# Streaming encoder step with PEER gathers: h for the dot products moved from PSUM to an SBUF copy, and the row ring from thirteen to twelve

## The reference, cut to what matters

```python
def peer(h, w_q, sub_keys, expert_u, expert_v):
    q = (t @ w_q).reshape(T, 8, 2, 64)
    s = jnp.einsum('thpd,hpnd->thpn', q, sub_keys)
    ts, ti = lax.top_k(s, 16)
    ...
    act = jax.nn.gelu(jnp.einsum('td,thkd->thk', xb, expert_u[idb]), approximate=False)
    return jnp.einsum('thk,thkd->td', gtb * act, expert_v[idb])
```

## Time and profile before

| | |
|---|---|
| runs | 3525.51, 3532.18, 3525.33 us |
| profiled execution, own time | 3508.12 us |
| its span, first to last instruction | 3505.7 us |
| mean granted TensorE clock | 0.825 |
| busy: PE / VectorE / GpSimd / ScalarE | 2387.2 / 2172.2 / 2141.8 / 259.9 us |
| gathers | 2176, 1140.99 MB, 86.0% of 16 DMA engines' span |

### The profile page before, as it was taken

One profiled execution on the slowest core, in us unless ns is written; L12 is line 12 of the kernel. 1 busy time (PEld: TensorE's weight loads), 2 busy tenths in 40 slices (PEclk: granted clock), 3 DMA queues, 4 the chain that ended last, 5 costly groups with the idle time before them and its releaser, 6 DMA issues.

```text
span 3505.7 us, 25147 instructions
## 1 busy us (share of the span) xinstructions
PE 2387.2 (68%) x7990; PEld 890.5 (25%) x7990; DVE 2172.2 (62%) x5644; ACT 259.9 (7%) x506; POOL 2141.8 (61%) x2184
## 2 busy tenths in 40 slices
PE   7123876577875875587978366748798764865498
PEld 6112323121311241123314121412332322111022
DVE  3988278866666775735467777772716787655500
ACT  3000100100000000000100100001010000000000
POOL 0365566656665655666566656565656675666665
PEclk9666898788987967798989688669899886878799
DMA  6587898999899989997897999799789899999998
GB/s 236 222 326 297 297 366 313 366 349 378 320 379 360 350 318 409 410 410 290 309 366 292 372 341 387 291 379 355 288 316 362 339 349 348 369 387 385 370 380 330
DMA packets 331598, 1201.44 MB, mean 343 GB/s; under 512 B 40898, under 2 KB 41290, under 8 KB 329418
## 3 DMA queue, kind: packets, MB, share of 16 engines
q0 software_dynamic: 313344, 1140.99, 86.0%
q1 hardware_dynamic: 17034, 49.94, 3.7%
q10 hardware_dynamic: 1088, 8.91, 0.6%
HBM read 1188.82 MB, written 10.87 MB: 342 GB/s over the span
## 4 chain that ended last, share of the span: by engine, by line
PE 23%; another core or an unknown queue 21%; POOL 18%; DVE 17%; issue 14%; DMA 5%; ACT 2%; ACTq 0%; DVEq 0%; POOLq 0%
POOL rows L590 18%; PE acc L974 11%; DVE rows L1420 8%; PE psA L807 4%; DMA rows<-in_expert_v,idsT 4%; PE psB L917 3%; PE psA L798 2%; DVE work L1149 1%; DMA rows<-in_expert_u,ids 1%; DVE work L1235 1%; DVE work L1228 1%; PE psB L834 1%; DMA w_in_sb<-in_w_in 1%; DVE work L1225 1%
## 5 line engine op out<-in xcount | busy, mean ns | idle before, releaser
L974 PE MATMUL acc<-rows,strip 128*32 128x512 f32 x4352 | 1558.1, 654 | 546.8 <-DMA rows<-in_expert_v,idsT 403.3
L1420 DVE CUSTOM_DVE_ANT_0 rows<-rows,psH 128x1024 f32<-128x1024 f32 x1088 | 1290.9, 1218 | 399.7 <-DMA rows<-in_expert_u,ids 296.3
L590 POOL DMA_INDIRECT rows<-in_expert_v,idsT x1088 | 1100.5, 1011 | 667.3 <-issue 268.3
L590 POOL DMA_INDIRECT rows<-in_expert_u,ids x1088 | 1040.3, 956 | 681.6 <-issue 317.3
L974 PEld LDWEIGHTS acc<-rows,strip 128*32 128x32 f32 x4352 | 349.1, 115 | 1633.3 <-issue 1038.4
L807 PE MATMUL psA<-hT,w_in_sb 128*128 128x128 f32 (+1 forms) x1280 | 203.1, 315 | 97.9 <-issue 97.1
L807 PEld LDWEIGHTS psA<-hT,w_in_sb 128*128 128x128 f32 x1280 | 190.6, 231 | 124.0 <-issue 124.0
L1149 DVE SCALAR_TENSOR_TENSOR work<-zbuf,chan,work 128x128 f32<-128x128 f32 (+1 forms) x870 | 215.2, 325 | 6.7 <-DVE work L1149 3.9
L798 PE MATMUL psA<-w_out_sb,hT 128*128 128x512 f32 x320 | 163.0, 651 | 32.7 <-ACTq L661 25.9
L1427 DVE TENSOR_TENSOR x_out<-acc,x_out 128x1024 f32<-128x1024 f32 (+1 forms) x10 | 12.2, 1221 | 266.0 <-PE acc L974 178.6
L917 PE MATMUL psB<-w_q_sb,hT 128*128 128x512 f32 x288 | 141.2, 640 | 31.7 <-remote 15.7
(11 more groups left out here) (181 smaller groups left out, 1287.5 us busy)
## 6 DMA issues: line engine op xcount, KB each, us to landing
rows<-in_expert_u,ids POOLq DMA_INDIRECT x1088
rows<-in_expert_v,idsT POOLq DMA_INDIRECT x1088
w_in_sb<-in_w_in ACTq DMA_DIRECT2D x4, 2176.0 KB, 17.6
w_in_sb<-in_w_in SPq DMA_DIRECT2D x4, 2176.0 KB, 18.6
w_out_sb<-in_w_out SPq DMA_DIRECT2D x2, 4096.0 KB
w_q_sb<-in_w_q SPq DMA_DIRECT2D x2, 4096.0 KB
x_out<-x_mid SPq DMA_DIRECT2D x10, 512.0 KB
x_mid<-x_mix SPq DMA_DIRECT2D x8, 512.0 KB
```

Of the source, the lines that this page charges most:

```text
L590: nc.gpsimd.indirect_dma_start(out=rows[:, j, :], out_offset=None, in_=table[:, :], in_offset=bass.IndirectOffsetOnAxis(ap=index, axis=0))\
L974: last = nc.tensor.matmul(acc[LS * a:LS * (a + 1), half:half + 512], strip[:, first:first + LS], rows[:, at % RING, half:half + 512], star ...
L1420: nc.vector.tensor_tensor_reduce(rows[:, j, :], rows[:, j, :], psH[:, :], 1.0, 0.0, ALU.mult, ALU.add, dots[:, r:r + 1]).then_inc(s_free[j ...
```

## The change

ScalarE copies `psH` into a new SBUF tile `h_rows` once per item, behind `turn_h`; `take_row` waits for that copy and reads `h_rows`. `turn_h` of the next item waits for the copy as well. The new tile takes 4 KB of each partition, as much as one slot of the ring; the ring goes to twelve slots.

```diff
-RING = 13
+RING = 12
...
+        h_rows = sb("h_rows", [P, D])
...
+        s_hk = sem("h_rows_kept")
...
+            def keep_h(n):
+                act.wait_ge(s_h, n + 1)
+                nc.scalar.copy(h_rows[:, :], psH[:, :]).then_inc(s_hk, 1)
...
             first_queries()
+            keep_h(0)
             mixer(0, FINISH)
             for n in range(ITEMS + 2):
                 for tick in range(TICKS):
+                    if tick == TURN_H and n + 1 < ITEMS:
+                        keep_h(n + 1)
                     for v in ended(n, tick, GELU):
...
             def turn_h(n):
                 if n:
                     pe.wait_ge(s_cT, n)
+                    pe.wait_ge(s_hk, n)
                 pe.wait_ge(s_hT2, n + 1)
...
                 if r == 0:
-                    dve.wait_ge(s_h, n + 1)
+                    dve.wait_ge(s_hk, n + 1)
                 landed(dve, ("u", n, r))
-                nc.vector.tensor_tensor_reduce(rows[:, j, :], rows[:, j, :], psH[:, :], 1.0, 0.0,
+                nc.vector.tensor_tensor_reduce(rows[:, j, :], rows[:, j, :], h_rows[:, :], 1.0, 0.0,
                                                ALU.mult, ALU.add, dots[:, r:r + 1]).then_inc(s_free[j], 1)
```

## The result

The changed kernel takes 3596.68 us (median of 4 runs, 3589.32 to 3604.38). The kernel before, run beside it on the same chip, takes 3528.85 us (4 runs, 3525.33 to 3548.66). The ratio is 1.0189 (95% interval 1.016 to 1.0217): slower by 1.9%, where 5.7% was forecast.

What follows compares the result with a forecast made beforehand. The prediction took the stream of 2176 gathers GpSimd issues as the kernel's clock. Profiled 3508.1 + 148 (net hold) + 9 (taps) + 41 (ring) = 3706 us, 3724 with the timed runs' 17.4; it said 3725, +5.7%, range 3560 to 3900.

Steps and rivals of the forecast that it cites:

- the first rule that the prediction cites from that section: VectorE instructions with two SBUF inputs contend with GpSimd instructions reading SBUF; those with at most one do not.
- Rival 1: Takes: the custom instruction reads its second operand without stopping GpSimd, leaving only the smaller ring's cost; 3566 us, 13%.
- Gross size: GpSimd's gathers: 400 us of holds in takes before any absorption, plus 9 us behind the taps.
- 748 gathers wait a mean of 0.535 us: Gathers starting inside takes: each take holds for 1.07 us, 1164 us of 3386, giving 400 us of waiting.
- the first 0.05 us lets gathers pass: Takes: a gather starting in a take's first 0.05 us is not held, shortening the hold to 1.07 us.
- Behind the taps: Runs of 27 taps: the third gather waits for the next take's end, 1.1 us later; eight such, +9 us.
- What takes it up: GpSimd's "remote" waits, read as a full DMA queue, absorb 252 of the 400 us of holds; net 148.
- While the DMA queue is full a late gather costs nothing: GpSimd's gathers: the reason given for 252 us of "remote" waits absorbing holds.
- Twelve slots: Ring one slot smaller: GpSimd stops one gather earlier in 32 holes, 1.27 us each, +41 us; bounds 0 and 113.
- Length of a take and copy: Takes as long from SBUF as from PSUM, 0 (bounds +73, -172 us); ScalarE's ten copies hidden, 0 (uncovered 20 us).
- rival 3: Takes: the SBUF form is shorter and holds nothing, so rows come free sooner; 3481 us, 3%.
- Rival 2: Chains of takes: gathers are held throughout, GpSimd runs freely only outside takes and taps; middle 3931 us, 15%.

Runs made afterwards that it cites:

- e4: Kernel before (thirteen slots, no copy) with each take multiplying the row by itself, two SBUF operands: 3377.26 us, 1.0558, at the faster level.
- e3: Changed kernel with each take multiplying PSUM's h by h_rows, one SBUF operand: 3222.22 us, 1.0069 against the kernel before.
- e15: Kernel before with each take multiplying the row by itself, thirteen slots, at the slower level: 3571.34 us, 1.0176.
- e7: Kernel before with each gather fetching half a row, 2 KB, at the slower level: 3490.94 us, 0.9946.
- e1: Kernel before with twelve slots and nothing else, at the faster level: 3217.4 us, 1.0059.
- e10: Kernel before with twelve slots alone, on another chip of the faster level: 1.0047.
- e14: Kernel before with twelve slots alone, at the slower level: 3515.55 us, 1.003.
- e2: Changed kernel with takes reading PSUM again, twelve slots and copy kept: 3215.52 us, 1.0045 against the kernel before.
- e11: The changed kernel itself on a chip of the faster level: 3395.39 us, 1.0586 against the kernel before.
- e6: Kernel before with the convolution taps' running sum in PSUM, only the last tap writing SBUF, slower level: 3460.51 us, 0.9874.
- e8: Kernel before with half-row gathers and each take multiplying the row by itself, two SBUF operands, slower level: 3618.44 us, 1.031.

## Why the prediction was right in direction and wrong in size

**The mechanism held.** Two SBUF operands hold a gather until 0.10 us before the take's end. e4 alone makes it, e3 with the same h_rows and one SBUF operand doesn't. In the changed kernel all 394 gathers that start 0.05 to 1.0 us into a take are held, none of the 87 that start at 1.12 us or later is. What is held is the start of a gather, not the whole of it. After its release a gather needs 0.91 us, nearly all of its 0.94, and the one released at 1304.21 spends 0.78 of them inside the next take, unhindered. Of 145 gathers that start 0.05 to 0.6 us ahead of a take in the changed kernel, 139 last at most 1.0 us; the other 6 start inside a TENSOR_TENSOR or SCALAR_TENSOR_TENSOR, as in the earlier trace rows. So the forecast goes too far where it says that this trace speaks against the inference of the Trainium skill (SBUF — State Buffer, "Who interferes with whom") that descriptor generation isn't disturbed: e4 against e3 (504 against 49 long gathers) shows that a two-input take holds a gather, not that it disturbs the writing of descriptors. A gather's index lies in an SBUF tile (`ids`, `idsT`). If a gather reads it at its start, the hold is the case of the first rule that the prediction cites from that section, a GpSimd instruction that reads SBUF. That fits the traces, but no run took the index out of SBUF, so it is not shown. Rival 1 (no hold) falls with the same pair.

**Gross size, 400 + 9 forecast, 345 measured.** The step that failed first is "748 gathers wait a mean of 0.535 us". It assumed starts spread evenly over a take. In the changed kernel they aren't: where takes stand back to back, a released gather ends 0.8 us into the next take (1305.12 in the take of 1304.34), so its follower starts at 1.08, just ahead of that take's end, where nothing is left to hold it. 877 gathers start inside a take, 383 of them at 1.00 to 1.12 us; all together lose 323 us, 0.37 each. That the first 0.05 us lets gathers pass was wrong in the other direction: 83 of 100 such were held, the one at 1301.16 among them. It had been taken from the taps.

**Behind the taps, +9 forecast.** Where a take follows a run of taps at once, the mechanism showed as told: the third gather now waits for the end of that take. It did so four times.

```profile
615.26 7.17 DVE L1159 SCALAR_TENSOR_TENSOR work<-zbuf,chan,work 128x128 f32<-128x128 f32 x27
616.45 1.02 POOL L592 DMA_INDIRECT rows<-in_expert_v,idsT  x1 [0.31 <-issue]
617.77 6.61 POOL L592 DMA_INDIRECT rows<-in_expert_u,ids  x1 [0.30 <-issue]
622.35 1.22 DVE L1430 CUSTOM_DVE_ANT_0 rows<-rows,h_rows 128x1024 f32<-128x1024 f32 x1
```

That is 1.13 us more than the 5.48 of the earlier trace rows. In the kernel before, six gathers over 2.1 us end where a take follows at once; the working counted eight. The four extra holds make only some 5 us. But there are 25 gathers over 2.1 us in place of 18, and their excess went from 88.8 to 116.6 us, +28: a term inside its bounds of 9 and 64, most of it from other gathers that came to start in a run of taps or of takes.

**What takes it up, 252 forecast, 282 measured in e15 (261 here, with the ring in it), and for another reason.** "While the DMA queue is full a late gather costs nothing" is the sentence that failed. e7 leaves the DMA engines idle nearly half the time and 291 us of "remote" waits stay; they are slots whose semaphore comes late. And at the level without "remote" waits, where this step would give 0 taken up and 400 net, 126 us are taken up all the same, from holes behind slots in use. The reading that fits both: a gather that comes late finds its slot free and its semaphore there, so every hole of whatever kind gives way. At the slower level e15 takes 145 us from "remote" and 111 from TensorE's slots. The forecast counted all of the first and none of the second, and landed near the sum for the wrong reason.

**Twelve slots, +41 forecast, +8 to 18 measured** (e1 18, e10 14, e14 8 us). The working let each of 32 holes keep its full 1.27 us. Its own lower bound, that later catching up hides part of it, is nearer. That is the next larger error after the gross size.

**The sum at this level.** Forecast +198 = 409 + 41 - 252. Measured in the traces +84 = 345 - 261, where -261 holds the ring too. So 64 of the 114 us too many come from the gross hold, 50 from what fills and from the ring; of those the ring explains some 33 (41 less the 8 of e14), the rest is the better filling of holes. Against the 68 us of the timed runs the forecast is 130 us too high.

**At the 3200 level the change costs 5.86%**, close to the 5.7% forecast, but that is no merit of it: there the terms are 302 gross, 126 taken up and 14 for the ring.

**Length of a take and copy, 0 and 0: right.** A take lasts 1225 against 1218 ns, 1088 x 0.007 = 8 us of VectorE's time. The lower fixed cost from SBUF that the Trainium skill gives (VectorE: DVE Perf Modes, section on the trn2 errata) doesn't show in 1225 against 1218, so rival 3 is out. The copies take what the earlier trace rows said, and e2 equals e1:

```profile
L693 ACT COPY h_rows<-psH 128x1024 f32<-128x1024 f32 x10 | 10.1, 1012 | 67.6 <-remote 56.7 <-issue 5.6 <-PE psH L768 5.3
```

**Rival 2 (chains of takes hold throughout) is out as a forecast, but its mechanism exists.** Of the gathers held in a take of the changed kernel all but two are let go at that take's own end and last 2.0 us at most. The two, at 1992.99 and 2918.75, start 0.05 us into a take and are held through the next one as well:

```profile
1992.94 1.20 DVE L1430 CUSTOM_DVE_ANT_0 rows<-rows,h_rows 128x1024 f32<-128x1024 f32 x1
1992.99 3.11 POOL L592 DMA_INDIRECT rows<-in_expert_u,ids  x1 [0.30 <-issue]
...
1994.08 1.21 DVE L1430 CUSTOM_DVE_ANT_0 rows<-rows,h_rows 128x1024 f32<-128x1024 f32 x1
```

In e11 one such gather (at 1912.32) lasts 6.55 us, through five takes that start 1.14 us apart, each before the one ahead has ended. Of the 107 gathers held in a take of the changed kernel behind which the next take starts that early, 105 are let go all the same.

## What to carry to other kernels

Where GpSimd issues indirect DMAs, look at every VectorE instruction that runs beside them for two SBUF operands, before looking at its own length; one operand in PSUM costs VectorE next to nothing here (1218 against 1225 ns a take, 349 against 345 ns a tap) and frees the gathers. Chains of short instructions hold a single gather longest, up to 17.0 us in the changed kernel; taking them out gave 1.3% (e6). Count the cost of a hold in the engine's busy time and what gives way in its idle time as two sums, and don't give an unexplained wait a cause to absorb things with until a run has taken that cause away. A net cost that hangs on slack differs from chip to chip (1.9 and 5.9% here), so the terms carry over, the sum doesn't.

## What the runs showed of the hardware

- The same kernel takes about 3200 us on some chips and about 3510 on others. At the slower level GpSimd has 335 us of "remote" waits (up to 6.9 us each), at the faster one none. Half the bytes (291 us stay) or twice the descriptor memory (305 us stay) don't remove them. They end on updates of a slot's semaphore that the trace has 1.7 to 12.5 us after the slot's last use, where the faster level has every one within 0.18 us; why, wasn't found.
- Gathers fall into step with the instructions that hold them, so the loss can't be taken from evenly spread starts: it was 0.37 us a start in the first 1.12 us of a take in the changed kernel, where 383 of 877 starts fall behind 1.00 us, and 0.49 us in e8, where 786 of 888 fall where the take holds.
- Gathers of 2 KB rows in place of 4 KB rows made the kernel only 0.5% faster (e7), while with held takes on top they cost 3.7% more (e8 against e7), twice the 1.8% at full rows on that level (e15). GpSimd's issue and its waits, not the bytes, are what this stream pays for.
- With the sum in PSUM the third gather passes in a chain of taps at 0.94 us, with it in SBUF it waits 5.5 to 6.6 us, though two gathers ahead of it pass in the same chain. The point within a tap at which a gather starts tells them apart: in the kernel before, 48 gathers start in chains of 128x128 taps; the 23 that pass start within 0.07 us of a tap's start or at least 0.17 us behind it, the 18 that last over 2.1 us 0.09 to 0.20 us behind it. Why that is so isn't shown.
